# Output projection of a hybrid decoder: the gated half's blocks one by one between the units of attention, the attended half after them

## The reference, cut to what matters

```python
y_ssm = _s5_mixer(u, ...)                  # width 1024, ends in a sigmoid gate
y_fox = _fox_attention(fq, fk, fv, ff)     # 8 heads of 64
y_dsa = _dsa_attention(dq, dk, dv, iq, ik, iw, topk)  # 8 heads of 64, 64 keys chosen per query
y = jnp.concatenate([_rms_norm(y_ssm, g_ssm), _rms_norm(y_fox, g_fox), _rms_norm(y_dsa, g_dsa)], axis=-1)
return y @ w_out                           # 2048 x 2048
```

## Time and profile before

| | |
|---|---|
| median of 3 runs | 2811.59 us (2807.5 to 2816.85) |
| the profiled execution: its time, its span | 2811.41 us, 2809.6 us |
| PE busy, weight loads busy | 95%, 91% of the span |
| DVE, ACT busy | 63%, 49% |
| from HBM | 397.5 MB, 142 GB/s over the span |
| chain that ended last | 89% PE, 6% DVE, 3% ACT |

### The profile page before, as it was taken

One profiled execution on the slowest core, in us unless ns is written; L12 is line 12 of the kernel. 1 busy time (PEld: TensorE's weight loads), 2 busy tenths in 40 slices (PEclk: granted clock), 3 DMA queues, 4 the chain that ended last, 5 costly groups with the idle time before them and its releaser, 6 DMA issues.

```text
span 2809.6 us, 56056 instructions
## 1 busy us (share of the span) xinstructions
PE 2668.1 (95%) x21786; PEld 2548.4 (91%) x21786; DVE 1782.2 (63%) x2890; ACT 1366.1 (49%) x2051; POOL 11.9 (0%) x19
## 2 busy tenths in 40 slices
PE   5989999989999999999979899999899999999997
PEld 5989866989999999999979898669899999999997
DVE  6777555576666666544487775655766666665445
ACT  5444443456555555433364444444566665653333
POOL 0000000000000000000000000000000000000000
PEclk8999975899999999999999999659999999999999
DMA  4433210435555555554444332104355555555553
GB/s 170 146 113 127 76 45 1 150 120 179 179 173 177 172 173 171 180 173 166 165 146 150 107 127 77 38 1 163 115 194 182 182 180 179 184 184 186 173 183 112
DMA packets 109728, 401.84 MB, mean 143 GB/s; under 512 B 12176, under 2 KB 12176, under 8 KB 109584
## 3 DMA queue, kind: packets, MB, share of 16 engines
q1 hardware_dynamic: 108432, 395.15, 41.9%
q0 software_dynamic: 1152, 4.63, 0.4%
HBM read 397.50 MB, written 2.23 MB: 142 GB/s over the span
## 4 chain that ended last, share of the span: by engine, by line
PE 89%; DVE 6%; ACT 3%; issue 2%; DMA 1%; SPq 0%; ACTq 0%; DVEq 0%
PE ps L383 25%; PE ps L384 25%; PE ps L385 25%; PE ps L587 2%; PE ps L554 2%; PE ps L530 1%; PE ps L456 1%; PE ps L522 1%; PE ps L575 1%; PE ps L543 1%; PE ps L465 1%; DVE h L1047 1%; DVE h L1067 1%; ACT h L715 1%; PE ps L531 1%
## 5 line engine op out<-in xcount | busy, mean ns | idle before, releaser
L699 ACT ACTIVATE w_hi<-raw 128x1024 fp32r<-128x1024 f32 x728 | 763.6, 1057 | 935.3 <-PE ps L385 918.0
L384 PE MATMUL ps<-x_lo,w_hi 128*128 128x272 f32 (+1 forms) x3904 | 1122.1, 287 | 0.0
L385 PE MATMUL ps<-x_hi,w_hi 128*128 128x272 f32 (+1 forms) x3904 | 1120.2, 287 | 0.0
L992 DVE TENSOR_TENSOR w_lo<-raw,w_hi 128x1024 fp32r<-128x1024 f32 x592 | 716.8, 1224 | 616.3 <-ACT w_hi L699 616.2
L383 PE MATMUL ps<-x_hi,w_lo 128*128 128x272 f32 (+1 forms) x2816 | 805.5, 286 | 19.9 <-DVE x_lo L1075 19.3
L384 PEld LDWEIGHTS ps<-x_lo,w_hi 128*128 128x128 f32 x3904 | 741.3, 190 | 1.8
L385 PEld LDWEIGHTS ps<-x_hi,w_hi 128*128 128x128 f32 x3904 | 741.1, 190 | 0.0
L383 PEld LDWEIGHTS ps<-x_hi,w_lo 128*128 128x128 f32 x2816 | 530.8, 189 | 21.8 <-issue 19.2
L383 PE MATMUL ps<-g_hi,w_lo 128*128 128x272 f32 (+1 forms) x1408 | 403.9, 287 | 4.8 <-DVE w_lo L992 2.7
L384 PE MATMUL ps<-g_lo,w_hi 128*128 128x272 f32 (+1 forms) x1408 | 403.2, 286 | 0.0
L385 PE MATMUL ps<-g_hi,w_hi 128*128 128x272 f32 (+1 forms) x1408 | 401.2, 285 | 0.0
(11 more groups left out here) (257 smaller groups left out, 2977.6 us busy)
## 6 DMA issues: line engine op xcount, KB each, us to landing
raw<-stream SPq DMA_DIRECT2D x744, 512.0 KB, 3.3
h<-x SPq DMA_DIRECT2D x4, 544.0 KB, 6.2
out<-h SPq DMA_DIRECT2D x4, 544.0 KB, 2.7
cst<-consts POOLq DMA_DIRECT2D x2, 724.0 KB, 6.4
wkv<-w_kv POOLq DMA_DIRECT2D x2, 512.0 KB, 7.8
b_st<-ssm_b POOLq DMA_DIRECT2D x2, 512.0 KB, 9.2
c_st<-ssm_c POOLq DMA_DIRECT2D x2, 512.0 KB, 11.4
par<-params SPq DMA_DIRECT2D x1, 562.0 KB, 12.0
```

The source lines that it names most:

```text
L384: pe.matmul(acc, w_hi[:, slot, kk, cols], lo, start=False, stop=False)
L385: mm = pe.matmul(acc, w_hi[:, slot, kk, cols], hi, start=False, stop=k == tiles - 1)
L699: act.activation(w_hi[:, slot, :, :], raw[:, slot, :, :], ACT.Copy).then_inc(hi_made, 1)
L992: dve.tensor_tensor(w_low(phase, slot), raw[:, slot, :, :], w_hi[:, slot, :, :].bitcast(F32), ALU.subtract).then_inc(in_lo_made if phase = ...
```

## The change

The output projection becomes two phases of the stream. "gated" has 8 groups of 2 blocks over the first 1024 rows of `w_out`, "out" 8 groups of 2 blocks over the other 1024. The 16 gated blocks are no longer in a loop of their own: block j stands behind the work of one unit on PE, in iterations 14, 16, 18 and so on to 44 (`gated_blocks`). ACT casts a block two iterations earlier, DVE makes its low part one iteration earlier and takes the residual of a group in the iteration after its second block. All gated groups use banks 0-1. The low parts have four places of their own (`gated_w`) in memory that is free by then. The residual of "gated" is the old one, that of "out" a single addition to `h`. The gated half is scaled in iterations 7 to 10 and split in 11 and 13, and the first attention's output transposes all use bank 2.

```diff
-PHASES = {"in": (17, DT // KB, 1), "glu": (4, UT // KB, 4), "out": (8, DT // KB, 4),
-          "up": (FT, DT // KB, 2), "down": (8, FT // KB, 4)}
-SPLIT = ("in", "out", "up", "down")
+PHASES = {"in": (17, DT // KB, 1), "glu": (4, UT // KB, 4), "gated": (8, UT // KB, 4),
+          "out": (8, UT // KB, 4), "up": (FT, DT // KB, 2), "down": (8, FT // KB, 4)}
+SPLIT = ("in", "gated", "out", "up", "down")
...
-Y_BANKS = (1, 2, 1, 4, 5, 6)
+Y_BANKS = (2, 2, 2, 4, 5, 6)
...
+GATED_FROM = 14
...
+def gated_blocks(n):
+    return [j for j in range(16) if j * (UNITS - 1 - GATED_FROM) // 16 == n - GATED_FROM]
...
+        gated_w = [place(f"gated_w{b}", [P, KB, 2 * P], F32R, at=a)[0] for b, a in enumerate(
+            (high + 4 * NT * IQ0, high + 4 * NT * IQ0 + 4 * KB * 2 * P, high + 4 * NT * FV0, e))]
...
-                                                 (ffn, end_at, lo_made, first_low(l, "out"))):
+                                                 (ffn, end_at, lo_made, first_low(l, "gated"))):
...
+            def gated_block(l, n):
+                g, b = n // 2, n % 2
+                if b == 0:
+                    pe.wait_ge(psum_free, first_group(l, "gated") + g + 2)
+                pe.wait_ge(lo_made, first_low(l, "gated") + n + 1)
+                split_block("gated", (first_block(l, "gated") + n) % SLOTS, b, 0, UT, lambda k: (y_hi[:, k, :], y_lo[0][:, k, :]),
+                            (lambda k: (ylo_made, 4 * l + k // 4 + 1)) if n < 2 else None)
...
                 pe.wait_ge(ynorm, 6 * l + n + 1)
-                if n == 2:
-                    pe.wait_ge(yt_made, 6 * l + 1)
+                if n in (1, 2):
+                    pe.wait_ge(yt_made, 6 * l + n)
                 for t in range(4):
...
                         output_transposes(l, 0, n - FOX_NORM - 8)
+                    for j in gated_blocks(n):
+                        gated_block(l, j)
...
                     output_transposes(l, 1, q)
...
-                products(l, "out", lambda k: (y_hi[:, k, :], y_lo[k // UT][:, k % UT, :]), lambda k: (ylo_made, 4 * l + k // 4 + 1))
+                pe.wait_ge(psum_free, first_group(l, "out") + 2)
+                products(l, "out", lambda k: (y_hi[:, UT + k, :], y_lo[1][:, k, :]), lambda k: (ylo_made, 4 * l + k // 4 + 3))
...
-                    if n in (GATE_NORM + 9, GATE_NORM + 13):
-                        high_part((n - GATE_NORM - 9) // 4)
+                    if n in (GATE_NORM + 6, GATE_NORM + 8):
+                        high_part((n - GATE_NORM - 6) // 2)
+                    for j in gated_blocks(n + 2):
+                        cast(l, "gated", j)
...
+                bank = 0 if phase == "gated" else 2 * (g % 2)
                 dve.wait_ge(block_used, first_block(l, phase) + blocks * (g + 1))
-                h2 = h[:, 2 * g:2 * g + 2, :]
-                dve.scalar_tensor_tensor(out=h2, in0=x_lo[:, 2 * g:2 * g + 2, :].bitcast(F32), scalar=ALPHA,
-                                         in1=ps[:, 2 * (g % 2):2 * (g % 2) + 2, 0:NT],
-                                         op0=ALU.mult, op1=ALU.add).then_inc(psum_free, 1)
-                dve.wait_ge(psum_free, first_group(l, phase) + g + 3)
-                mark(dve.scalar_tensor_tensor(out=h2, in0=x_hi[:, 2 * g:2 * g + 2, :].bitcast(F32), scalar=ALPHA, in1=h2,
-                                              op0=ALU.mult, op1=ALU.add))
-                if g < PIVOT // 2:
+                h2, acc = h[:, 2 * g:2 * g + 2, :], ps[:, bank:bank + 2, 0:NT]
+                if phase == "out":
+                    dve.tensor_tensor(h2, h2, acc, ALU.add).then_inc(psum_free, 1)
+                    dve.wait_ge(psum_free, first_group(l, phase) + g + 3)
+                else:
+                    dve.scalar_tensor_tensor(out=h2, in0=x_lo[:, 2 * g:2 * g + 2, :].bitcast(F32), scalar=ALPHA,
+                                             in1=acc, op0=ALU.mult, op1=ALU.add).then_inc(psum_free, 1)
+                    dve.wait_ge(psum_free, first_group(l, phase) + g + 3)
+                    mark(dve.scalar_tensor_tensor(out=h2, in0=x_hi[:, 2 * g:2 * g + 2, :].bitcast(F32), scalar=ALPHA, in1=h2,
+                                                  op0=ALU.mult, op1=ALU.add))
+                if g < PIVOT // 2 and phase != "gated":
...
-                    if GATE_NORM + 4 <= n < GATE_NORM + 12:
-                        k = n - GATE_NORM - 4
-                        last = dve.scalar_tensor_tensor(out=yssm[:, k, :], in0=yssm[:, k, :], scalar=param("mix_g", l * DT + k),
-                                                        in1=rstd[:, :], op0=ALU.mult, op1=ALU.mult)
+                    if GATE_NORM + 4 <= n < GATE_NORM + 8:
+                        for k in range(2 * (n - GATE_NORM - 4), 2 * (n - GATE_NORM - 4) + 2):
+                            last = dve.scalar_tensor_tensor(out=yssm[:, k, :], in0=yssm[:, k, :], scalar=param("mix_g", l * DT + k),
+                                                            in1=rstd[:, :], op0=ALU.mult, op1=ALU.mult)
                         if k % 4 == 3:
...
-                    if n in (GATE_NORM + 13, GATE_NORM + 17):
-                        low_y((n - GATE_NORM - 13) // 4)
+                    if n in (GATE_NORM + 8, GATE_NORM + 10):
+                        low_y((n - GATE_NORM - 8) // 2)
+                    for j in gated_blocks(n + 1):
+                        low_part(l, "gated", j)
+                    for j in gated_blocks(n - 1):
+                        if j % 2:
+                            residual(l, "gated", j // 2)
...
-                for g in range(8):
-                    for n in range(4):
-                        if g:
-                            low_part(l, "out", 4 * g + n)
-                    if g:
+                for g in range(1, 9):
+                    for n in range(2):
+                        if g < 7:
+                            low_part(l, "out", 2 * g + 2 + n)
+                    if g < 8:
```

More of the change, by code:

```diff
@@ L73, in first_low @@
 def first_low(layer, phase):
-    mine = ("in",) if phase == "in" else ("out", "up", "down")
+    mine = ("in",) if phase == "in" else ("gated", "out", "up", "down")
     size = {p: PHASES[p][0] * PHASES[p][1] for p in mine}
@@ L256, in w_low @@
         def w_low(phase, slot):
-            return in_lo[slot // 2][:, slot % 2, :, :] if phase == "in" else w_lo[:, slot, :, :]
+            if phase == "in":
+                return in_lo[slot // 2][:, slot % 2, :, :]
+            return gated_w[slot][:, :, :] if phase == "gated" else w_lo[:, slot, :, :]
         def rope_bank(r):
@@ L314, in _ @@
             for l in range(DEPTH):
-                mixer, gates, ffn = (first_block(l, p) + SLOTS for p in ("in", "glu", "out"))
+                mixer, gates, ffn = (first_block(l, p) + SLOTS for p in ("in", "glu", "gated"))
                 end_at = min(first_block(l + 1, "in") + SLOTS, DEPTH * BLOCKS_PER_LAYER)
@@ L1631, in lay_out @@
         stream.append(blocks_of(i["ssm_glu_w"][l]))
-        stream.append(blocks_of(i["w_out"][l]))
+        stream.append(blocks_of(i["w_out"][l][:SSM_W]))
+        stream.append(blocks_of(i["w_out"][l][SSM_W:]))
         stream.append(blocks_of(i["w_up"][l].reshape(D_MODEL, 2, FT, P).transpose(0, 2, 1, 3).reshape(D_MODEL, -1)))
```

## The result

The kernel got slower. Its median of five runs is 2826.91 us (2825.94 to 2829.55), against 2812.32 us for the kernel before on the same chip; the ratio is 1.0052, with a 95% interval of 1.0037 to 1.0067. That is a loss of 14.6 us where 7 us of gain were forecast. The profiled execution took 2827.17 us, 15.8 us more than that of before.

The account below looks back on a forecast made before the run. PE at half clock was taken to bound attention. Per layer +25.1 and +9.0 (attentions), -48.6 (projection), -0.7, +0.5 make -14.7 us; cold blocks' 11.4 leave -3.3, -6.6 in all: 2805 us from 2811.41, range 2774 to 2850.

Parts of the forecast that it names:

- the way to the layer norm: Last residual before the layer norm: one operation instead of two on the path, -0.7 us per layer.
- the block's price: Each of the 16 gated blocks among the attention units costs 3.04 us at full clock.
- the number of cold blocks: Six blocks per layer in attention start at half clock (first, four at long gaps, one more), 1.9 us each, 11.4 us.
- the projection's gain: Sixteen blocks leave the output projection, saving 48.6 us per layer.
- every block cold: Rival for attention: all 16 blocks start at half clock, +15.7 us per layer, 2843 us, slower; chance 0.26.
- The gap in iterations 37 and 38: Second attention: PE waits for DVE's bank 2 read behind low part and residual, 6.8 us instead of 3.6.
- Small terms: Per layer: last residual -0.7 us, scaling in four iterations instead of eight +0.5 us, extra instructions nothing visible.
- cheaper values: Attention units at 1.05 us with the clock staying up: some 5 us more gain, the range's low end of 2774.
- the gaps of 2.9 and 3.6 us: Two units between blocks in second attention: DVE's work makes the gap 2.9 us, 3.6 us with a residual.
- the three named waits: In attention PE waits for low_part and residual before gated blocks, bank 2's read before transposes of iterations 36 and 37.
- The clock stays up: Rival for attention: full clock from the first block on, -14.7 us per layer, 2782 us; chance 0.20.
- Room at any clock: Rival: array free outside weight loads, blocks add only 24.1 us to attention, -24.7 us per layer, 2762 us; chance 0.05.

Follow-up runs that it names:

- e5: The changed kernel with the pivot made earlier on PE and three pivot subtractions on DVE put before group 6's residual: 2818.81 us, ratio 1.0026.
- e3: The changed kernel with each gated block's cast and low part made one iteration earlier: 2797.96 us, ratio 0.9953.
- e9: The changed kernel with the edits of e2, e3 and e5, attended low parts reordered, top-k rounds in even iterations and the sparse bias earlier: 2752.22 us, ratio 0.9783.
- e1: The changed kernel with the pivot made earlier on PE and residuals before the second low part: 2828.77 us, ratio 1.0057.
- e8: The changed kernel with four dense matmuls into bank 2 added in odd iterations 15 to 43 but 35, 37 and 39: 2822.43 us, ratio 1.0038.
- e2: The changed kernel with the first attention's output transposes two iterations apart: 2805.22 us, ratio 0.9974.

## Why the prediction was wrong

The mechanism in attention was right: dense blocks bring the clock up, the units shrink, and what room that makes is taken by DVE's work and by cold starts. The step that failed is the way to the layer norm, which the sum had at -0.7 us and which came out at +3.3; besides it the block's price, the number of cold blocks and the projection's gain were each set 1.7 to 2.5 us too well. The forecast's margin was only 3.3 us a layer between terms of 49 and 46 us, so the sign came out wrong. The measured time lies in the wide range, between the forecast and the case "every block cold", but outside the 2793 to 2817 us that the forecast gave itself for three to nine cold blocks. By its steps, per layer, with 11.3 us to explain (+8.0 against -3.3):

- **The way to the layer norm, -0.7 forecast, +3.3 measured.** I took an operation off the path and didn't ask what a group of half the length does to the DVE work that stands between the last two residuals. e5 shows it: with the subtractions moved, the pause is 14.23 us, 0.5 less than before, which is near the 0.7 forecast. Some 1.5 us of the lengthening are the sums at the half clock, which e3 was spared with the same wait. 4.0 of the 11.3 us.
- **A block, 3.04 forecast, 3.2 measured.** 24 matmuls 0.125 us apart are 3.0 us, so the rate was right; the first and the last matmul of a block take 0.1 us longer each, 0.2 a block. 16 x 0.16 = 2.5 us over the forecast.
- **Cold blocks, six by 1.9 forecast, eight by 1.65 measured**, 13.2 instead of 11.4 us. All five that were named were cold (the first, and those of iterations 18, 24, 36 and 38: numbers 0, 2, 5, 11 and 12). For the "one more" there were three, 4, 10 and 14, behind gaps of 3.43, 3.26 and 3.68 us with a residual in them, while 6 and 8, behind 3.61 and 3.68 us, were not. The prediction's second rival was to decide "from about eight cold blocks". There were eight, but by 13.2 against 14.7 us they alone don't turn the sign.
- **The gap in iterations 37 and 38, 6.8 forecast, 8.3 measured.** The wait was as said; but the clock fell during it, so the transposes and unit 38 ran at the half clock. The one before 36 was forecast at 5.7 and measured 5.68. Another 1.1 us came from the first unit, 14, which took 2.6 us and not 1.5, since it still ran at the half clock; the other gaps were shorter than forecast by as much in sum.
- **The projection, -48.6 forecast, -46.9 measured.** A wait of 0.79 us for `attended_lo` in the first block wasn't foreseen: before, the attended half's rows met PE in a group's later blocks. Of the other 0.9, 0.6 are the rate: the 94.0 us that were divided by 742 also held eight matmuls of the layer norm, which stay. Without them matmuls start 0.125 us apart, so 16 blocks are 48.0 us, not 48.6.
- **Small terms.** The scaling cost 0.7 us (forecast 0.5), and the stretch behind unit 47 was 0.5 us shorter.

Together 4.0 + 2.5 + 1.8 + 1.5 + 1.7 + 0.2 - 0.5 = 11.2.

Two slips in the prediction changed nothing. The page's two low slices are 7 and 5 in the first layer, but 6 and 5 in the second. And the ends of the range don't follow from the cases named for them: every block cold at 2.4 us gives 2811.4 + 2 x (16 x 2.4 - 14.7) = 2859 us, not 2850, and cheaper values 2777, not 2774.

What held: the gaps of 2.9 and 3.6 us (2.6 to 3.1 and 3.3 to 3.7 measured), the units at full clock (two in 2.2 to 2.9 us in e9, against 2.5), the three named waits, the absence of any wait for ACT's cast or a load. Of the forecast's checks, the projection came at 53 instead of 51 us, attention at 129.9 instead of 124, its mean clock at 0.85 (0.80 and 0.88 in its two stretches), as forecast.

The rivals. *The clock stays up* was false here. In e9, with the long gaps and the waits for DVE gone, it holds for all blocks but the first, and the 98.2 us for units 14 to 47 are under the 113 us of that case. *Every block cold* was half true, 8 of 16. The Trainium skill, "TensorE: Matmul & The Clock Gate", section "HAM oscillation", says that waits between bursts let the clock fall so that each burst starts cold. Here the trace agrees where a wait was long (bank 2, sparse bias, the round of `top_scores`), and with all waits gone in e9 the cold starts went too; but blocks 4 and 10 show that the clock can be low behind a gap with little waiting as well. *Room at any clock* was false: the blocks were paid in full, and room came from the clock alone. The Trainium skill, "Perfetto Trace Analysis", section "Identifying the Most-Contended Engine", would have given the 24.5 us without weight loads as headroom. No run here shows such headroom; in e9 the weight loads are busy for 82.7 of 98.2 us and PE for 96.8.

What stays open: what exactly makes the clock fall at a gap of 3.3 to 3.7 us. In the first layer of e1, with the same gaps, it was blocks 8 and 14 that were cold and not 4, 10 and 14; in its second layer it was 4, 10 and 14 again. The same instructions with the same gaps thus give either, from one layer to the next.

## What to carry to other kernels

If long, dense pieces of one engine are laid between short dependent steps, they are also the cover for the other engines' work: put what the next step needs *under* the dense piece, one iteration earlier. DVE idled under the blocks and was then waited for; moving its work, with the clashes on bank 2 and at the layer norm taken out, brought 2826.9 us to 2752.2 us. When a stage is cut to half its length, list the work of the other engines that its length used to hide, above all at its end. And where two terms of 50 us leave 3 us over, the sign isn't known: each term under 1 us that is repeated 16 times belongs in the sum.

## What the hardware showed that was not expected

- **The clock can fall inside dense work.** In e3 block 2 starts at the full clock after a wait of 1.34 us and loses it 1.3 us later, with no pause between its matmuls; they start 0.125 us apart, then 0.23:

```profile
431.57 0.39 PE L393 MATMUL ps<-y_hi,gated_w 128*128 128x272 f32 x1 [1.34 <-DVE h L1112]
...
432.68 0.28 PE L395 MATMUL ps<-y_hi,w_hi 128*128 128x272 f32 x1
432.80 0.33 PE L393 MATMUL ps<-y_hi,gated_w 128*128 128x272 f32 x1
...
433.15 0.43 PE L395 MATMUL ps<-y_hi,w_hi 128*128 128x272 f32 x1
433.38 0.43 PE L393 MATMUL ps<-y_hi,gated_w 128*128 128x272 f32 x1
```

  The only pause near it is the one ahead of the block. So where a stretch is cold, look at the gap ahead of it too, and not only at the work in which it shows; that the gap is the cause was not shown by a run.
- **More work on the bound engine need not take more time.** e8 adds four matmuls (0.7 us) to each of 12 gaps a layer, 8 us a layer, and its five executions, 2820.82 to 2824.75 us, all lie under the five of the changed kernel. Part of the filler fell into waits for DVE, and fewer blocks were cold; how much of the latter is the filler's doing is open, as said above.
- **One long wait costs more than its length.** The two waits for bank 2 are 6.4 us in a layer; without them (e2) the first layer is 10.3 us shorter: 7.3 us in the two gaps, and 3.3 us in blocks 11 and 12, which then found the full clock.
